# An unread tile of 224 bytes ahead of the coefficient tiles

## The reference

```python
h = x @ w_in[l] + b_in[l]                        # 2048 -> 5120
a = silu(layer_norm(causal_dwconv31(a_val * sigmoid(a_gate))))
s = sc_b * causal_dwconv3(sc_c * sc_h)
y = concatenate([a, s]) @ w_out[l] + b_out[l]    # 2048 -> 2048
x = layer_norm(ALPHA * x + y)
q = x @ w_q                                      # 2048 -> 2048
...                                              # 16 of 16384 experts for each of 8 heads
act = gelu(einsum('td,thkd->thk', x, u_sel), approximate=False)
f = einsum('thk,thkd->td', act * g, v_sel)
x = layer_norm(ALPHA * x + f)
```

## Time and profile before

| | us |
|---|---|
| median of 3 runs | 1748.53 (1746.63 to 1752.34) |
| span of the profiled execution | 1745.8 |
| TensorE busy | 1713.3 (98%) |
| VectorE busy | 1407.6 (81%) |
| ScalarE busy | 854.0 (49%) |
| GpSimd busy | 540.4 (31%) |
| DMA, mean over the span | 289 GB/s |

### The profile page before, as it was taken

The page is one execution under the profiler, slowest core; times in us unless marked ns, Lnnn a source line. Parts: engine busy times, 40 slices in busy tenths (PEclk is TensorE's granted clock), DMA queues, the critical chain, the costliest instruction groups (busy, mean ns, idle before and its releaser), DMA issues.

```text
span 1745.8 us, 31461 instructions
## 1 busy us (share of the span) xinstructions
PE 1713.3 (98%) x11910; PEld 1578.1 (90%) x11910; DVE 1407.6 (81%) x1998; ACT 854.0 (49%) x1084; POOL 540.4 (31%) x342
## 2 busy tenths in 40 slices
PE   8999999899999999999999999999999999999997
PEld 8999987799999999999999999998788777878776
DVE  7999997678967677777777777556899898999997
ACT  5544436344544444444444444445555555555544
POOL 0000000288881000000000000004787777777731
PEclk9999999999999999999999999999999999999999
DMA  7787787777777777777677777899899999999994
GB/s 267 267 276 267 234 260 249 273 237 235 250 249 252 238 236 244 247 235 239 237 241 239 236 244 243 282 355 332 314 400 400 399 401 389 400 399 395 369 398 133
DMA packets 173728, 504.52 MB, mean 289 GB/s; under 512 B 19408, under 2 KB 35920, under 8 KB 172624
## 3 DMA queue, kind: packets, MB, share of 16 engines
q1 hardware_dynamic: 134000, 427.08, 70.0%
q0 software_dynamic: 22528, 67.19, 10.0%
q10 hardware_dynamic: 17120, 9.35, 1.8%
HBM read 490.98 MB, written 79.69 MB: 327 GB/s over the span
## 4 chain that ended last, share of the span: by engine, by line
PE 78%; DMA 6%; DVE 6%; issue 5%; POOL 3%; ACT 1%; DVEq 1%; SPq 0%; POOLq 0%; ACTq 0%
PE psum L1411 18%; PE psum L1413 18%; PE psum L1412 18%; PE psum L1587 6%; PE psum L1589 6%; PE psum L1588 6%; POOL sp_coef L588 2%; DVE w_lo L843 2%; DMA raw<-in_v_w_dram 2%; PE psum L1553 2%; DMA raw_late<-in_v_w_dram 1%; PE psum L1460 1%; PE psum L1462 1%; PE psum L1461 1%; DVE psum L1312 1%
## 5 line engine op out<-in xcount | busy, mean ns | idle before, releaser
L627 ACT ACTIVATE w_hi<-raw 128x1024 fp32r<-128x1024 f32 x547 | 578.9, 1060 | 682.1 <-PE psum L1413 487.1
L1411 PE MATMUL psum<-xt_hi,w_hi 128*128 128x256 f32 x2944 | 827.2, 281 | 5.3 <-DVE xt_lo L857 3.1
L1412 PE MATMUL psum<-xt_lo,w_hi 128*128 128x256 f32 x2944 | 822.6, 279 | 0.0
L1413 PE MATMUL psum<-xt_hi,w_lo 128*128 128x256 f32 x2944 | 822.4, 279 | 0.0
L843 DVE TENSOR_TENSOR w_lo<-raw,w_hi 128x1024 fp32r<-128x1024 f32 x479 | 581.8, 1222 | 221.5 <-ACT w_hi L627 219.7
L1411 PEld LDWEIGHTS psum<-xt_hi,w_hi 128*128 128x128 f32 x2944 | 554.3, 188 | 6.6 <-issue 6.0
L1412 PEld LDWEIGHTS psum<-xt_lo,w_hi 128*128 128x128 f32 x2944 | 554.3, 188 | 0.0
L1413 PEld LDWEIGHTS psum<-xt_hi,w_lo 128*128 128x128 f32 x2944 | 554.1, 188 | 0.0
L582 POOL DMA_INDIRECT rows<-v_rows,sp_idx x96 | 130.9, 1364 | 709.7 <-issue 674.9
L1587 PE MATMUL psum<-w_hi,c_hi 128*128 128x512 f32 x752 | 299.7, 399 | 8.9 <-DVE w_lo L843 8.7
L1589 PE MATMUL psum<-w_hi,c_lo 128*128 128x512 f32 x752 | 298.2, 396 | 0.0
(11 more groups left out here) (164 smaller groups left out, 1131.8 us busy)
## 6 DMA issues: line engine op xcount, KB each, us to landing
raw<-in_u_w_dram SPq DMA_DIRECT2D x256, 512.0 KB, 4.2
raw<-in_v_w_dram SPq DMA_DIRECT2D x148, 512.0 KB, 8.7
v_rows<-in_v_w_dram SPq DMA_DIRECT2D x128, 512.0 KB, 5.2
raw_late<-in_v_w_dram SPq DMA_DIRECT2D x108, 512.0 KB, 8.9
raw<-in_w_in_dram SPq DMA_DIRECT2D x80, 512.0 KB, 4.3
raw<-in_w_out_dram SPq DMA_DIRECT2D x32, 512.0 KB, 4.5
raw<-in_w_q_dram SPq DMA_DIRECT2D x32, 512.0 KB, 4.5
hid_spill<-hid ACTq DMA_DIRECT2D x7, 1024.0 KB, 15.4
```

The costliest lines, as they stand in the source:

```text
L627: nc.scalar.activation(parts_of(slot_u)[0][:, :], raw_of(slot_u), ACT.Copy).then_inc(hi_done, 1)
L1411: mm(dst, hi_w[:, sl], xt_hi[:, kk, :], start=st, stop=False)
L1412: mm(dst, hi_w[:, sl], xt_lo[:, kk, :], start=False, stop=False)
L1413: i = mm(dst, lo_w[:, sl], xt_hi[:, kk, :], start=False, stop=en)
```

## The change

A tile of 56 float32 for a partition, 224 bytes, is put between `neg_mean` and the first coefficient tile. Nothing writes or reads it. Every tile allocated behind it moves up by 224 bytes; `raw`, `w_hi`, `w_lo` and the four small tiles stay. All line numbers below L192 grow by one; no instruction changes its operation, its operands' shapes or its place in an engine's order.

```diff
         mv = sb("mv", [P, TB, 2], f32)
         rstd = sb("rstd", [P, TB, 1], f32)
         neg_mean = sb("neg_mean", [P, TB, 1], f32)
+        sb("place_pad", [P, 56], f32)
 
         def coefs(name, where):
```

## The result

The changed kernel took **1778.37 us** (median of 4 runs, 1773.12 to 1780.77) against 1749.43 us for the kernel before in as many runs beside it: a ratio of 1.0155, 95% interval 1.0136 to 1.0173. It is slower, by about 29 us. The forecast was 1712.5, in a range of 1701 to 1750.

A forecast was written before the change was run, and what follows sets the result against it. TensorE hardly waits, so the number of matmuls times their step was taken to bound the kernel. Gains of 4.5 + 1.5 + 2.6 + 20.5 + 2.7 + 3 + 1.2 = 36.0 us took 1748.5 to 1712.5, range 1701 to 1750.

The forecast's parts named there:

- The natural experiment in the trace: Last units of the down projection: 512-column steps of 226.7 ns with tail, 233.7 with w, attributed to the weights' place.
- the rival in which the tail's far place helps: Down projection: tail streams faster because it lies over 130 KB further on; w stays, so 1748.5 us; chance 0.15.
- The step that failed: 256-column matmuls: the tail's saving of 16 clocks in 512 columns, taken as the same share, gives 3.33 ns each.
- The tail's 6.8 ns: Last units of the down projection: 512-column step of 233.4 with w less 226.6 ns inside the tail stretches.
- the ends are nothing and all 10 ns: 256-column matmuls: bounds on the saving for each, with 3.33 ns taken between them.
- Mixer input, query, up: Three stages of 256-column matmuls: gains of 4.5, 2.6 and 20.5 us from 3.33 ns each, part of the first kept back.
- Mixer output 1.5: Mixer output, 235 to 328 us: 384 x 6.8 = 2.6 us, of which 1.5 was taken.
- Down projection 2.7 + 3 + 1.2: Down projection: gains before, within and after the 1280 to 1680 us DMA plateau; 15.3 us if TensorE alone set the pace.
- Slower: the place at 0 is the bad one: All stages: each operand at offset 0 costs one clock in 32, giving 120.0 and 240.0 ns, 1790 us; chance 0.09.
- only 512: 256-column stages stay at 116.7 ns, held by weight loads; only 512-column matmuls gain 8.4 us, 1740 us; chance 0.08.
- no change: Whole kernel: absolute rather than relative place matters, so the time stays at 1748.5 us; chance 0.15.
- The rule that spoke against: TensorE: the skill's two independent read ports mean relative position cannot matter, so the summed gain would be zero.

The follow-up runs named there:

- the second kernel: Against the changed kernel, small tiles moved last and pads put xt back at 288, mix, c and tail at 0: 1746.93 us, ratio 0.9973 to the kernel before.
- the first experiment: Against the kernel before, the four small tiles put ahead of raw with no pad, so only the weights moved, to equal offsets: 1776.1 us, ratio 1.0138.

## Why the prediction was wrong

- **The natural experiment in the trace** was read rightly and gave what it could: 512 columns went from 233.3 to 226.7 ns with c and with `mix`, as forecast, and the rival in which the tail's far place helps fell with that, since `w` stayed where it was.
- **The step that failed** is "since the loss before was the same share in both widths, I take the same share off 256 columns: 3.33 ns". The size was exact and the sign was wrong: the step went from 116.7 to 120.0, not to 113.3. 8832 x 3.33 = 29.4 us, as much as the whole result. The equal share, 9.4% in both widths, was a coincidence of one offset; at 64 the two forms have 113.3 and, stationary, 233.3. The tail's 6.8 ns had been measured on one form only, and the two forms differ in more than width: in one the weights stand still and `xt` streams, in the other the weights stream. Which of the two differences matters was not separated. And "the ends are nothing and all 10 ns" bounded a gain alone. No row showed a 256-column matmul with float32 operands at equal offsets, so nothing bounded a loss either; it was left to a rival at 0.09 and kept out of the range.
- The nearest row of 256 columns spoke for a gain: gate matmuls, equal offsets, 115 ns by the prediction's reading. In the changed kernel they take what they took (277 ns each by the records), beside 120.0 a step for the float32 ones, so a 16-bit matmul says nothing on a 32-bit one here. "That is weaker" was right, and it was still counted for.
- **Mixer input, query, up** (4.5 + 2.6 + 20.5 us of gain): a loss of 6.3 and 22.4 us instead. That these stages feel TensorE's step in full was right for query and up. In the mixer the forecast kept 1.9 of 6.4 us back for a new wait for `w_lo` or `mix_lo`; the change, being slower there, could not show it, but where the step was 113.3 ns it came: the mixer's input was 5.5 us shorter (220.2 against 225.7), and the wait for `mix_lo` grew from 1.1 to 3.1 us.
- **Mixer output 1.5**: 2.0 measured.
- **Down projection 2.7 + 3 + 1.2**: the faster step came, and none of the time in the profile; the stage took 2.1 us more, which lies inside the 8 us by which the profiles of this stage differ. The mechanism was named rightly, DMA at its plateau with VectorE beside it and the rest turning "into these same waits", and the two kernels without the gathers agree with it: 15 us there. The size of 6.9 us was too high by the best measure on record: the second kernel gained 2 to 7 us in all, 2 of them in the mixer, which leaves 0 to 5 for this stage. Two products are 0.1 us off (1665 x 6.8 is 11.3, 190 x 6.8 is 1.3), which changes nothing.
- **Slower: the place at 0 is the bad one** gave 120.0 ns for 256 columns, which is what came, and 240.0 for 512, which did not. Its 1790 us were nearer than the forecast's 1712.5, but that was luck: with places counted absolutely no operand lies at 0 in the first experiment, so its rule gives 113.3 ns there, where 120.0 were measured. The **only 512** rival had the wrong sign as well, and **no change** missed the loss.
- The rule that spoke against: the runs show a step that depends on where one operand lies against the other, between 113.3 and 120.0 ns for the same instruction. By the Trainium skill (TensorE: Matmul & The Clock Gate, Step-by-step: what each phase is for) weight loads and the streaming operand have read ports of their own, and loading the next weights takes no read bandwidth from the running matmul. Read as "the place makes no difference" it would have given 1748.5 us for the change, and the steps measured here do not agree with that reading; whether the two reads are what meets, no run shows.

What remains open is why: no run tells what inside the chip makes equal offsets good for one form and bad for the other, nor what it is in the end of a gate batch, in a wait or in a few transposes that picks the pace.

## What to carry to other kernels

Where TensorE is never idle, measure the step of each form of matmul by itself, and do not carry a step from one form to another (other width, other operand standing still, other type), however well the percentages agree: if no row shows the new combination, a loss belongs in the range as much as a gain. Place is a parameter of such a kernel: try the offset between the stationary and the streaming tiles for each form by itself, in steps of 32 bytes, and look at the step both ahead of and behind every wait and every other kind of matmul in between. And before a faster step is counted, look whether DMA and the engines that feed TensorE leave room: here at least 10 of its 15 us vanished in a stage with DMA near 400 GB/s.

## What the runs showed of the hardware

- At a granted clock of 1.00 the step of a float32r matmul of 256 columns was 113.3 to 120.0 ns and that of one of 512 columns 226.7 to 234.4 ns, by the offset between the two operands modulo 512 bytes and, for 256 columns, by what TensorE had done before. An estimate from these steps: 8832 x 6.7 ns = 59 us, 3% of this kernel.
- Within one trace the 512-column step alternated between 233.3 and 227.1 ns with the place of the stationary operand, at 288 and at 0.
- At 64, 192 and 320 bytes the 256-column step has two lasting values, 113.3 and 117.8 ns. At 192, behind an uncut batch of 16-bit matmuls it was 117.8; behind one whose last matmul was cut in 128 and 128, or in 192 and 64, 113.3; behind one whose last two were cut, 117.8. In one execution it went from 113.3 to 117.8 ns behind a wait of 0.44 us for `w_lo`. The same code in the mixer had either, in different executions.
- The same cut at 288 bytes changed nothing (116.7 ns, ratio 1.0008).
- DMA stood at 395 and 394 GB/s over 400 us of the down stage in the kernel before and the changed one, whether TensorE's step was 233.3 or 226.7 ns; single slices of its plateau read 369 to 403.
